# Output projection with its second half in two passes, two expert weight loads placed between them, and expert choice for two token tiles at a time

## The chip, the cores and the metric

The kernel runs on one core of one Trainium2 chip. The metric is the device time of one execution in microseconds (us); the result is the median over several runs. The engines are PE (TensorE, matrix products), PEld (its weight loads), DVE (VectorE), ACT (ScalarE), POOL (GpSimd) and SP (SyncE, which here only issues DMA transfers).

## The reference

One layer of a decoder trunk on 512 tokens of width 1024, all in float32. Only the middle of it matters here:

```python
x = x + (merged @ w_out)                     # output projection, 1024 x 1024
h = rmsnorm(x) * g_ffn
lg = h @ w_router_g + b_rg                   # 4 groups: the best one is taken
le = h @ w_router_e + b_re                   # 8 experts in each: the best two of that group
wts = p_g * softmax(top2(le[group]))
for each token, for its two experts e:       # 32 experts, hidden width 256
    out += (silu(h @ w_gate[e]) * (h @ w_up[e])) @ w_down[e] * wts
```

Ahead of it stand an input projection with attention, convolution and mLSTM branches; behind it a per-layer embedding and a last RMSNorm.

## The kernel before

The program is written engine by engine: each engine has one instruction stream in a fixed order, and semaphores tie the streams together. So every order spoken of below is written out by hand.

**Output projection.** `project(i)` computes, for i = 0 to 7, 512 output columns (half i // 4) of the token tile i % 4 of 128 tokens. Each operand is split into a rounded high part and a low remainder, so one tile takes 24 matrix products of 128x128 by 128x512: `by_part` lists them as high x high (part 0), high x low weights (part 1), low merged x high weights (part 2), 8 each. The four banks PA, PB, S_1 and S_4 take the tiles in turn. DVE adds the result to the residual (`add_x2`), PE transposes it (`turn_half`), DVE multiplies by the gain (`h2_half`) and PE computes the router's logits (`router`). All of that runs between pieces of the next tile's projection.

**Choice of experts.** `pick(t)` on DVE takes the logits of one tile: scale and bias, best group, mask, best two of 32, one-hot rows `oh`, and their sum `tmp`. `row_root` finishes the RMSNorm's reciprocal root with five small instructions ahead of it. PE counts tokens per expert from `tmp` (the banks RANKS for tiles 0 and 1, LAST_RANKS for tiles 2 and 3), DVE turns the counts into slots (`ranked`), PE sums a table of token numbers by slot (HIT), and DVE writes it out as `table`. POOL then gathers the tokens of each expert, 64 at a time, from the copy of x in memory (`x2_rows`). The weights of the tokens follow: a chain of small DVE instructions, and PE's products HIT_WEIGHT. Only behind these, in PE's order, stands the first `turn_block`, which transposes the gathered rows of expert 0.

**Experts.** Each of 32 experts loads 2048 KB (`up_weights`) and 1024 KB (`down_weights`). There are 7 places for up weights (`RING`) and 9 for down weights (`DOWN_RING`). They lie in memory that earlier stages used. Place 4 for up weights lies on `merged_low`, place 3 for down weights on the last four k tiles of `wo_low` for the second half, place 5 on `wo_high` of the second half, place 4 for down weights on the first four k tiles of its `wo_low`. SP issues the load of up n (n from 7 on) once `up_done` says that expert n - 7 has left its place. SP's stream after the projection's first half reads:

```python
            sp.wait_ge(x2_mm, T)
            up_weights(2)
            up_weights(3)
            ...
            sp.wait_ge(x2_mm, 2 * T)
            store_x2(T - 1)
            down_weights(3)
            down_weights(4)
            up_weights_in_halves(4)
            up_weights_in_halves(5)
```

Of the kernel before, what the change touches and what calls it, by code (L numbers as in the profile page):

```python
# [31 lines left out]
ALU = mybir.AluOpType  # L32
# [3 lines left out]
P = 128  # L36
# [87 lines left out]
def build(nc, x, consts, chan, g_mix, r_bias, g_final, w_cm, w_tm, w_if, w_gate, w_branch, w_out,  # L124
# [5 lines left out]
    with ExitStack() as ctx:  # L130
# [6 lines left out]
        def sem(name):  # L137
            return ctx.enter_context(nc.semaphore(name))
# [168 lines left out]
        best = sb("best", [P, T, 8])  # L307
        best_at = sb("best_at", [P, 8], mybir.dt.uint32)
        best_index = sb("best_index", [P, 8])
        ov = sb("ov", [P, 3, NEXP])  # L310
# [123 lines left out]
        wo_loaded = sem("wo_loaded")  # L434
        x2_mm = sem("x2_mm")
        x2_ready = sem("x2_ready")
        x2_squared = sem("x2_squared")
# [63 lines left out]
        def _(sp):  # L501
# [87 lines left out]
            up_weights(2)  # L589
            up_weights(3)  # L590

            def store_x2(t):
# [80 lines left out]
        def _(act):  # L673
# [288 lines left out]
            for i in range(2 * T):  # L962
# [6 lines left out]
                if i >= T:  # L969
# [3 lines left out]
                                   bias=mean_halves[:, t:t + 1]).then_inc(rooted, 1)  # L973
            act.wait_ge(picked, T)
            act.activation(t4[:, :, :], t4[:, :, :], ACT.Exp).then_inc(act_step, 1)
# [109 lines left out]
        def _(pe):  # L1085
# [249 lines left out]
            last_tile_last = sorted(by_part, key=lambda q: (q[1] == KD - 1, q))  # L1335

            def project(i, first=0, end=3 * KD):

                half, tokens = i // T, slice(i % T * P, (i % T + 1) * P)
                bank = (PA, PB, S_1, S_4)[i % 4]  # L1340
                if i >= T and first == 0:
                    pe.wait_ge(x2_ready, i - 3)
                if i == T:
                    pe.wait_ge(rounded, WO_REST_ROUNDED + KD)
                for n, (part, k) in list(enumerate(last_tile_last if i == 0 else by_part))[first:end]:
                    if i == 0 and part == 0:
                        pe.wait_ge(rounded, MERGED_ROUNDED + k + 1)
                    if i == 0 and part == 1 and k in (0, KD - 1):
                        pe.wait_ge(gate_split, WO_SPLIT + KD)
                    if i == 0 and part == 2:  # L1350
                        pe.wait_ge(gate_split, MERGED_SPLIT + k + 1)
                    if i == T and n == KD:
                        pe.wait_ge(gate_split, WO_REST_SPLIT + KD)
                    last = mm(bank[:, :], (merged_high, merged_high, merged_low)[part][:, k, tokens],
                              (wo_high[half][:, k, :], wo_low[:, half, k, :], wo_high[half][:, k, :])[part],
                              n == 0, n == 3 * KD - 1)
                if end == 3 * KD:
                    last.then_inc(x2_mm, 1)
# [39 lines left out]
            for i in range(1, T + 1):  # L1398
                project(i, 0, 4)
                turn_half(i - 1)  # L1400
                project(i, 4, 10)
                router(i - 1)
                project(i, 10)
            for i in range(T + 1, 2 * T):
                project(i, 0, 4)
                turn_half(i - 1)
                if i < 2 * T - 1:
                    project(i, 4, 10)
                else:
                    project(i, 4, 8)  # L1410
                    pe.wait_ge(picked, 2)
                    mm(RANKS, const("upper"), tmp[:, 0:2, :], True, False)
                    mm(RANKS[:, NEXP:], ones, tmp[:, 0, :], False, True).then_inc(routing_mm, 1)
                    project(i, 8, 10)
                router(i - 1)
                project(i, 10)

# [16 lines left out]
            for q in range(2):  # L1434
                mm(LAST_RANKS, ones, tmp[:, q, :].unsqueeze(1).to_broadcast([P, 2, NEXP]), q == 0, False)
            pe.wait_ge(picked, 3)
            mm(LAST_RANKS[:, NEXP:], ones, tmp[:, 2, :], False, False)

# [11 lines left out]
            constant_products(3)  # L1450
            pe.wait_ge(picked, T + 1)
            mm(LAST_RANKS, const("upper"), tmp[:, 2:T, :], False, True).then_inc(routing_mm, 1)
            constant_products(3)
# [64 lines left out]
            for n in range(NEXP):  # L1518
                pe.wait_ge(up_loaded[n % RING], (n // RING + 1 + (n % RING in (4, 5))) * 16)
# [85 lines left out]
        def _(dve):  # L1605
# [414 lines left out]

            def pick(t, meanwhile):

                of = lambda q: per[:, q, 0, t:t + 1]
                groups, experts, left = rl[:, t, 0:NGROUP], rl[:, t, NGROUP:], le[:, t, :]
                dve.wait_ge(logits_done, T + t + 1)
                chain(dve.scalar_tensor_tensor(rl[:, t, :], logits_in(t, 1), rr2[:, t:t + 1], r_b[:, :], ALU.mult, ALU.add))
                if t < T - 1:
                    chain(dve.scalar_tensor_tensor(rl[:, t, :], logits_in(t, 0), rr2[:, t:t + 1], rl[:, t, :], ALU.mult, ALU.add))
                first_max(groups, const("rev4"), oh4[:, t, :], of(1), of(11))
                last = dve.tensor_scalar(t4[:, t, :], groups, of(1), None, ALU.subtract)  # L2030
                if t == T - 1:
                    last.then_inc(picked, 1)
                chain(dve.tensor_scalar(oh4[:, t, :], oh4[:, t, :], of(11), 1.0, ALU.is_equal, ALU.subtract))
                chain(dve.scalar_tensor_tensor(left.rearrange("p (g e) -> p g e", g=NGROUP),
                                               spread(oh4[:, t, :], [P, NGROUP, PER_GROUP], 2), BIG,
                                               experts.rearrange("p (g e) -> p g e", g=NGROUP), ALU.mult, ALU.add))
                chain(dve.max(best[:, t, :], left))
                chain(dve.max_index(best_at[:, :], best[:, t, :], left))
                chain(dve.tensor_copy(best_index[:, 0:2], best_at[:, 0:2]))
                chain(dve.tensor_scalar(oh[:, 0, t, :], numbers, best_index[:, 0:1], None, ALU.is_equal))  # L2040
                meanwhile()
                dve.scalar_tensor_tensor(tmp[:, t, :], numbers, best_index[:, 1:2], oh[:, 0, t, :], ALU.is_equal, ALU.add)\
                   .then_inc(picked, 1)
                chain(dve.tensor_scalar(oh[:, 1, t, :], numbers, best_index[:, 1:2], None, ALU.is_equal))
                dve.tensor_tensor(entries_ids.rearrange("p (k t) w e -> p k t w e", k=2)[:, :, t],
                                  oh[:, :, t, :].unsqueeze(2).to_broadcast([P, 2, 2, NEXP]),
                                  const("ids").rearrange("p (k t w) -> p k t w", k=2, w=2)[:, :, t, :].unsqueeze(3)
                                  .to_broadcast([P, 2, 2, NEXP]), ALU.mult)

# [367 lines left out]
```

## Time and profile before

| | |
|---|---|
| median of 3 runs | 944.79 us |
| lowest, highest | 941.2 us, 945.15 us |
| span of the profiled execution, first to last instruction | 939.8 us |
| PE busy | 895.7 us (95%) |
| DVE busy | 497.7 us (53%) |
| ACT busy | 343.9 us (37%) |
| POOL busy | 194.1 us (21%) |
| bytes read, written | 175.33 MB, 12.59 MB |

The profiled execution has a span of 939.8 us. Its own device time is not listed beside it; the three timed runs lie 1.4 to 5.4 us above that span. A busy share is a mean over stages with different limits. The stages that matter here are the projection (574 to 630 us from the start), the choice of experts (630 to 648 us) and the experts (648 to 868 us).

### The profile page before, as it was taken

Reading aid. Unit: us, or ns where it says so; the run is one execution under the profiler, and the core shown is the slowest. Engines: PE = TensorE matmul, PEld = TensorE weight load, DVE = VectorE, ACT = ScalarE, POOL = GpSimd, SP = SyncE. Lnnn points to the kernel's source line nnn. Section 1 sums busy time; section 2 is a strip of 40 time slices with the busy share of each in tenths; the row PEclk is TensorE's granted clock in tenths of the full one; section 3 lists DMA queues with packets and bytes.
Section 4 is the critical chain, followed back from the end, with each engine's and each line's share of the span. In section 5 each row is a group of like instructions: output and inputs, shape, how many; then the busy total and the mean of one; then the engine's idle time right before and its main releaser. Section 6 shows DMA issues by size and latency. Waiting matters only on the chain. (4 is left out here: it accounts for less than half of the span.)

```text
span 939.8 us, 12274 instructions
## 1 busy us (share of the span) xinstructions
PE 895.7 (95%) x4824; PEld 656.4 (70%) x4824; DVE 497.7 (53%) x1039; ACT 343.9 (37%) x571; POOL 194.1 (21%) x169
## 2 busy tenths in 40 slices
PE   5999999999999999899999999997999999878897
PEld 4778788878877866788888888885555555433486
DVE  6378579758866978743333344374311221211766
ACT  5534453535445347622222234120222212112565
POOL 0052263327225332000000000002233233221000
PEclk9999999999999999999999999999999999999999
DMA  7520321222031110442222208959999999999801
GB/s 277 177 93 23 130 73 45 70 89 68 23 113 45 68 35 0 182 199 101 101 100 101 101 1 326 402 186 381 412 419 419 419 419 421 419 421 413 313 24 68
DMA packets 28657, 180.35 MB, mean 192 GB/s; under 512 B 5792, under 2 KB 6304, under 8 KB 17848
## 3 DMA queue, kind: packets, MB, share of 16 engines
q1 hardware_dynamic: 23480, 171.16, 46.4%
q0 software_dynamic: 5120, 8.41, 2.4%
q8 instruction: 39, 0.64, 0.3%
q14 instruction: 18, 0.15, 0.0%
HBM read 175.33 MB, written 12.59 MB: 200 GB/s over the span
## 5 line engine op out<-in xcount | busy, mean ns | idle before, releaser
L1087 PE MATMUL bank<-mT_parts,low_parts 128*128 128x512 f32 (+1 forms) x456 | 178.5, 394 | 0.0
L1087 PE MATMUL bank<-arena,cst 128*64 128x256 f32 (+2 forms) x920 | 134.1, 431 | 9.7 <-DMA arena<-in_w_expert 7.2
L1087 PE MATMUL bank<-mT_parts,x_parts 128*128 128x512 f32 (+1 forms) x328 | 132.5, 404 | 1.0 <-DVE low_parts L1676 1.0
L1087 PE MATMUL bank<-hT_parts,x_parts 128*128 128x512 f32 (+1 forms) x328 | 129.1, 394 | 0.0
L1676 DVE TENSOR_TENSOR low_parts<-arena,x_parts 128x1024 fp32r<-128x1024 f32 (+1 forms) x44 | 62.8, 1427 | 98.1 <-ACT x_parts L702 97.8
L2150 DVE TENSOR_TENSOR cst<-bank,chn 128x512 f32<-128x512 f32 x32 | 22.1, 692 | 166.7 <-PE bank L1480 166.7
L1087 PEld LDWEIGHTS bank<-arena,cst 128*64 128x64 f32 (+1 forms) x920 | 63.7, 138 | 65.1 <-issue 31.5
L1087 PEld LDWEIGHTS bank<-mT_parts,low_parts 128*128 128x128 f32 (+1 forms) x456 | 85.0, 186 | 21.2
L1728 DVE SCALAR_TENSOR_TENSOR arena<-arena,chn 128x512 f32<-128x512 f32 x116 | 99.2, 912 | 0.0
L2301 POOL DMA_INDIRECT mT<-x_rows,table x32 | 33.0, 1031 | 274.8 <-DVE table L2080 262.2
L1087 PE MATMUL bank<-arena 128*128 128x64 f32 (+9 forms) x400 | 79.9, 332 | 1.2 <-DVE small L1825 1.2
L2286 POOL TENSOR_TENSOR arena<-arena 128x128 f32<-128x128 f32 (+3 forms) x32 | 40.3, 1260 | 177.7 <-ACT arena L798 177.7
L1087 PEld LDWEIGHTS bank<-mT_parts,x_parts 128*128 128x128 f32 (+1 forms) x328 | 61.0, 186 | 17.0 <-DVE low_parts L1676 2.1
L1087 PEld LDWEIGHTS bank<-hT_parts,x_parts 128*128 128x128 f32 (+1 forms) x328 | 61.0, 186 | 15.1 <-issue 0.7
L1087 PEld LDWEIGHTS bank<-arena 128*128 128x128 f32 (+1 forms) x400 | 56.3, 189 | 21.5 <-issue 14.3
L2307 POOL DMA_INDIRECT expert_rows<-mT,table x32 | 32.4, 1014 | 150.9 <-ACT mT L995 146.3
L798 ACT ACTIVATE arena<-arena,small 128x384 f32<-128x384 f32 (+3 forms) x32 | 32.6, 1020 | 55.8 <-DVE small L1825 55.8
L1087 PE MATMUL bank<-mT_parts,cm_high_b 128*128 128x512 f32 x128 | 51.6, 412 | 0.0
L939 ACT ACTIVATE arena<-bank 128x512 f32<-128x512 f32 x24 | 14.2, 597 | 100.6 <-PE bank L1087 96.2
L1087 PE MATMUL bank<-hT_parts,cm_high_b 128*128 128x512 f32 x128 | 49.2, 393 | 0.0
L995 ACT ACTIVATE mT<-bank,table_weight 128x512 f32<-128x512 f32 x32 | 22.0, 687 | 67.0 <-PE bank L1087 67.0
L1087 PE MATMUL bank<-x_parts,mT_parts 128*128 128x384 f32 x128 | 44.6, 349 | 0.0
(300 smaller groups left out, 1574.7 us busy)
## 6 DMA issues: line engine op xcount, KB each, us to landing
arena<-in_w_expert SPq DMA_DIRECT2D x21, 2048.0 KB, 26.5
arena<-in_w_expert SPq DMA_DIRECT2D x26, 1024.0 KB, 23.7
arena<-in_w_cm SPq DMA_DIRECT2D x32, 512.0 KB, 3.6
arena<-in_w_gate SPq DMA_DIRECT2D x8, 1536.0 KB, 6.7
yT<-in_w_expert SPq DMA_DIRECT2D x5, 2048.0 KB, 22.9
hT<-in_w_expert SPq DMA_DIRECT2D x4, 2048.0 KB, 25.0
arena<-in_w_tm SPq DMA_DIRECT2D x4, 1536.0 KB, 7.0
arena<-in_w_branch SPq DMA_DIRECT2D x8, 768.0 KB, 8.2
```

Of the source, the lines that this page charges most:

```text
L798: act.activation(sc[:, u % 2, 0:n], sc[:, u % 2, 0:n], ACT.Exp, bias=nmx[:, u % 2:u % 2 + 1], accum_out=den[:, u:u + 1]).then_inc(exps_don ...
L939: act.activation(sgm[:, br], (PA, PB, S_16)[br][:, :], ACT.Sigmoid).then_inc(gate_read, 1)
L995: act.activation(yr[slot], Y[b2][:, :], ACT.Copy, scale=table_w(0, n)).then_inc(y_scaled, 1)
L1087: return pe.matmul(out, lhsT, rhs, start=start, stop=stop)
L1676: dve.tensor_tensor(low, weights, high.bitcast(F32), ALU.subtract).then_inc(done, 1)
L1728: dve.scalar_tensor_tensor(cacc[:, j % 2], ypad[:, j:j + SEQ], weight, cacc[:, j % 2], ALU.mult, ALU.add).then_inc(conv_step, 1)
L2150: dve.tensor_tensor(xT[b2], TR[:, :].rearrange("p (k h s) -> p k h s", k=KD // 2, h=2), chn[:, G_FFN:G_FFN + KD].rearrange("p (h k) -> p k ...
L2286: pool.tensor_tensor(dst[:, 0:n], sc[:, u % 2, 0:n], sc[:, u % 2, n:2 * n], ALU.add).then_inc(pool_step, 1)
L2301: pool.indirect_dma_start(out=xr[slot], out_offset=None, in_=x2_halves, in_offset=bass.IndirectOffsetOnAxis(ap=token_halves, axis=0), boun ...
L2307: pool.indirect_dma_start(out=expert_halves, out_offset=bass.IndirectOffsetOnAxis(ap=row_halves, axis=0), in_=yr[slot], in_offset=None, bo ...
```

## The change

The second half of the projection is done in two passes over its four tiles. The first pass does 12 of the 24 products of every tile (all of part 2, then k tiles 4 to 7 of part 1), and leaves four unfinished sums in the four banks. A new semaphore `low_mm` says that it is over; `merged_low` and half of `wo_low` are then free. SP waits for it right behind `up_weights(3)`, and issues `up_weights(4)` (now whole) and `down_weights(3)` there. The second pass does the other 12 products of each tile. `pick` takes two tiles at once, `pick(0)` and `pick(2)`: some of its instructions now cover both tiles, others stand there twice. The call for the first two tiles stands ahead of `add_x2` of the last tile; the last pair needs both roots and `ranked(0, ...)` ahead of it.

```diff
@@ SP @@
             sp.wait_ge(x2_mm, T)
             up_weights(2)
             up_weights(3)
+            sp.wait_ge(low_mm, 1)
+            up_weights(4)
+            down_weights(3)
...
             store_x2(T - 1)
-            down_weights(3)
             down_weights(4)
-            up_weights_in_halves(4)
             up_weights_in_halves(5)
@@ PE @@
+            low_first = [(2, k) for k in range(KD)] + [(1, k) for k in range(KD // 2, KD)]
+            second_half = low_first + [(1, k) for k in range(KD // 2)] + [(0, k) for k in range(KD)]
+            LOW = len(low_first)
...
+                if i == 2 * T - 1 and end == LOW:
+                    last.then_inc(low_mm, 1)
...
-                project(i, 10)
+                project(i, 10, LOW if i == T else 3 * KD)
             for i in range(T + 1, 2 * T):
-                project(i, 0, 4)
-                turn_half(i - 1)
...
-                router(i - 1)
-                project(i, 10)
+                project(i, 0, LOW)
+            project(T, LOW)
+            project(T + 1, LOW, LOW + 5)
+            turn_half(T)
+            project(T + 1, LOW + 5)
+            project(T + 2, LOW, LOW + 1)
+            router(T)
...
+            turn_half(T + 2)
+            project(T + 3, LOW + 5)
...
-            constant_products(2)
+            router(2 * T - 2)
             turn_half(2 * T - 1)
-            constant_products(1)
+            pe.wait_ge(picked, 2)
+            mm(RANKS, const("upper"), tmp[:, 0:2, :], True, False)
+            mm(RANKS[:, NEXP:], ones, tmp[:, 0, :], False, True).then_inc(routing_mm, 1)
             router(2 * T - 1)
@@ DVE, pick @@
+                chained_by_tile(lambda t: dve.scalar_tensor_tensor(rl[:, t, :], logits_in(t, 1), rr2[:, t:t + 1], r_b[:, :],
+                                                                   ALU.mult, ALU.add), tiles)
+                chained_by_tile(lambda t: dve.scalar_tensor_tensor(rl[:, t, :], logits_in(t, 0), rr2[:, t:t + 1], rl[:, t, :],
+                                                                   ALU.mult, ALU.add), [t for t in tiles if t < T - 1])
+                once_read()
+                chain(dve.tensor_reduce(of(1), groups, AXX, ALU.max))
...
+                chained_by_tile(lambda t: dve.max(best[:, t, :], le[:, t, :]), tiles)
+                chained_by_tile(lambda t: dve.max_index(best_at[:, t - first, :], best[:, t, :], le[:, t, :]), tiles)
...
+                dve.tensor_tensor(tmp[:, pair, :], oh[:, 0, pair, :], oh[:, 1, pair, :], ALU.add).then_inc(picked, 2)
@@ DVE, the calls @@
-            for t in range(T - 1):
-                h2_half(T + t)
-                row_root(t)
-                if t == T - 2:
-                    ranked(0, RANKS, 1)
-                pick(t, lambda: add_x2(T + t + 1))
+            h2_half(T)
+            add_x2(T + 1)
+            row_root(0)
+            h2_half(T + 1)
+            add_x2(T + 2)
+            row_root(1)
+            pick(0, lambda: h2_half(T + 2))
+            add_x2(T + 3)
...
             h2_half(2 * T - 1)
+            row_root(T - 2)
             row_root(T - 1)
-            pick(T - 1, lambda: None)
+            ranked(0, RANKS, 1)
+            pick(T - 2, lambda: None)
```

Two places in the order of instructions show what moves.

PE, from the last tile of the projection (512 columns wide, operands `wo_low`, `wo_high`, `merged_low`, `mT_parts`) to its router products (128x36), before:

```order
L1087 MATMUL bank<-wo_high_62,mT_parts 128x512 x4
L1087 MATMUL bank<-tmp,cst 128x64
L1087 MATMUL bank<-tmp,cst 128x32
L1087 MATMUL bank<-wo_low,mT_parts 128x512 x2
L1087 MATMUL bank<-wr_sb,cst 128x36 x4
L1087 MATMUL bank<-wo_low,mT_parts 128x512 x6
L1087 MATMUL bank<-wo_high_62,merged_low 128x512 x8
L1087 MATMUL bank<-cst 128x128 x2
L1380 MATMUL bank<-cst,x_sb 128x128 x4
L1087 MATMUL bank<-cst 128x128
L1087 MATMUL bank<-wr_sb,cst 128x36 x4
```

The same place in the changed program:

```order
L1389 MATMUL bank<-cst,x_sb 128x128 x4
L1089 MATMUL bank<-wo_high_62,mT_parts 128x512 x7
L1089 MATMUL bank<-wr_sb,cst 128x36 x4
L1389 MATMUL bank<-cst,x_sb 128x128 x4
L1089 MATMUL bank<-tmp,cst 128x64
L1089 MATMUL bank<-tmp,cst 128x32
L1089 MATMUL bank<-wr_sb,cst 128x36 x4
```

The third tile's router products and the two products into RANKS (128x64 and 128x32) now stand behind the last product of the projection, and the three constant products around the last transposes are gone.

DVE, from the last two pieces of `add_x2` (128x256) to the last tile's router row (`rl`), before:

```order
L1979 TENSOR_TENSOR x_sb<-x_sb,bank 128x256 x2
L2042 SCALAR_TENSOR_TENSOR tmp<-cst,best_index,oh 128x32
L2044 TENSOR_SCALAR oh<-cst,best_index 128x32
L2045 TENSOR_TENSOR cst<-oh,cst 128x2x64
L1989 TENSOR_TENSOR cst<-bank,chn 128x256 x2
L1637 TENSOR_SCALAR small<-small 128x1
...
L1645 TENSOR_TENSOR small<-small 128x1
L2026 SCALAR_TENSOR_TENSOR rl<-bank,small,r_b 128x36
```

The same place in the changed program:

```order
L2083 TENSOR_TENSOR cst<-oh,cst 128x2x64 x2
L1992 TENSOR_TENSOR x_sb<-x_sb,bank 128x256 x2
L2002 TENSOR_TENSOR cst<-bank,chn 128x256 x2
L1650 TENSOR_SCALAR small<-small 128x1
...
L1658 TENSOR_TENSOR small<-small 128x1
L2028 TENSOR_TENSOR rank_terms<-bank,oh 128x128
L2030 TENSOR_REDUCE per<-rank_terms 128x2x2
L2031 TENSOR_TENSOR cst<-per,cst 128x2x128
L2054 SCALAR_TENSOR_TENSOR rl<-bank,small,r_b 128x36 x2
L2056 SCALAR_TENSOR_TENSOR rl<-bank,small,rl 128x36
```

The whole of `pick(0)` stands ahead of the last `add_x2`, two `row_root` of five instructions stand behind it where there was one, and the three instructions of `ranked(0, ...)` have come in between them and the last pair's choice.

## Rows read from the trace of the kernel before

**Rows 1.** Timeline of SP's DMA issues (start us, us, engine, line), 630 to 653 us

```profile
630.60 0.32 SPq L594 DMA_DIRECT2D x_rows<-x_sb  x1
...
652.96 0.33 SPq L559 DMA_DIRECT2D arena<-in_w_expert  x1
```

**Rows 2.** Windows by stage: length, busy PE PEld DVE ACT POOL, granted clock, DMA share, GB/s

```profile
613.00:632.00 19.00, 18.55 (x100) 14.97 (x99) 15.29 (x68) 3.43 (x10) 0.00 (x0) 1.00 0.41 154
632.00:653.00 21.00, 16.99 (x145) 11.47 (x145) 10.40 (x45) 1.33 (x3) 5.25 (x5) 0.92 0.99 389
657.00:810.00 153.00, 153.00 (x1118) 79.26 (x1116) 31.25 (x82) 31.97 (x72) 48.04 (x47) 1.00 1.01 418
810.00:868.00 58.00, 46.22 (x302) 21.75 (x299) 7.67 (x20) 9.90 (x22) 12.10 (x12) 1.00 1.01 420
```

**Rows 3.** PE's timeline, 600 to 657 us; a product is recorded as one or two instructions

```profile
603.79 0.98 PE L1087 MATMUL bank<-wr_sb,cst 128*128 128x36 f32 x8
604.61 1.66 PE L1087 MATMUL bank<-wo_low,mT_parts 128*128 128x512 f32 x6
606.10 2.01 PE L1087 MATMUL bank<-wo_high,merged_low 128*128 128x512 f32 x8
607.95 1.10 PE L1087 MATMUL bank<-wo_high,mT_parts 128*128 128x512 f32 x4
...
635.62 0.43 PE L1087 MATMUL bank<-tmp,cst 128*128 128x64 f32 x2 [0.83 <-DVE tmp L2042]
...
637.21 0.69 PE L1087 MATMUL bank<-cst 128*64 128x64 f32 x16 [0.44 <-DVE cst L2018]
637.83 1.08 PE L1087 MATMUL bank<-tmp,cst 128*128 128x32 f32 x8
638.74 4.54 PE L1087 MATMUL bank<-cst 128*128 128x512 f32 x10
643.21 1.15 PE L1087 MATMUL bank<-mT,cst 128*64 128x64 f32 x32
646.23 0.66 PE L1480 MATMUL bank<-cst,mT 128*128 128x128 f32 x4 [1.86 <-DMA mT<-x_rows,table]
647.76 5.17 PE L1087 MATMUL bank<-arena,cst 128*64 128x256 f32 x32 [0.88 <-DVE cst L2150]
...
656.52 1.95 PE L1087 MATMUL bank<-yT,cst 128*64 128x256 f32 x16
```

**Rows 4.** Half-microsecond windows, the same columns: the granted clock, and the DMA queues run dry

```profile
648.00:648.50 0.50, 0.50 (x4) 0.32 (x4) 0.00 (x0) 0.00 (x0) 0.50 (x1) 0.50 1.00 393
...
653.00:653.50 0.50, 0.50 (x4) 0.27 (x3) 0.00 (x0) 0.49 (x1) 0.00 (x0) 1.00 0.19 74
```

**Rows 5.** DVE's timeline, 625 to 636 us

```profile
625.34 0.29 DVE L2015 TENSOR_TENSOR rank_terms<-bank,oh 128x128 f32<-128x128 f32 x1
...
626.37 0.26 DVE L2026 SCALAR_TENSOR_TENSOR rl<-bank,small,r_b 128x36 f32<-128x36 f32 x1
626.66 0.26 DVE L2028 SCALAR_TENSOR_TENSOR rl<-bank,small,rl 128x36 f32<-128x36 f32 x1
...
629.77 0.75 DVE L1979 TENSOR_TENSOR x_sb<-x_sb,bank 128x256 f32<-128x256 f32 x2 [0.59 <-PE bank L1087]
...
631.75 0.20 DVE L1637 TENSOR_SCALAR small<-small 128x1 f32<-128x1 f32 x1
...
632.74 0.26 DVE L2026 SCALAR_TENSOR_TENSOR rl<-bank,small,r_b 128x36 f32<-128x36 f32 x1
...
633.68 0.23 DVE L2030 TENSOR_SCALAR t<-rl,per 128x4 f32<-128x4 f32 x1
633.81 0.23 DVE L2033 TENSOR_SCALAR oh<-oh,per 128x4 f32<-128x4 f32 x1
...
635.31 0.25 DVE L2042 SCALAR_TENSOR_TENSOR tmp<-cst,best_index,oh 128x32 f32<-128x32 f32 x1
```

**Rows 6.** POOL's timeline: the first gather

```profile
639.13 1.26 POOL L2301 DMA_INDIRECT mT<-x_rows,table  x1 [262.18 <-DVE table L2080]
```

More of the change, by code:

```diff
@@ L435, in build @@
         x2_mm = sem("x2_mm")
+        low_mm = sem("low_mm")
         x2_ready = sem("x2_ready")
@@ L1342, in project @@
                     pe.wait_ge(x2_ready, i - 3)
-                if i == T:
+                if i == T and first == 0:
                     pe.wait_ge(rounded, WO_REST_ROUNDED + KD)
-                for n, (part, k) in list(enumerate(last_tile_last if i == 0 else by_part))[first:end]:
+                order = second_half if i >= T else last_tile_last if i == 0 else by_part
+                for n, (part, k) in list(enumerate(order))[first:end]:
                     if i == 0 and part == 0:
@@ L1402, in _ @@
                 router(i - 1)
-                project(i, 10)
+                project(i, 10, LOW if i == T else 3 * KD)
             for i in range(T + 1, 2 * T):
-                project(i, 0, 4)
-                turn_half(i - 1)
[L1407 to L1414, printed above, removed]
-                router(i - 1)
-                project(i, 10)
+                project(i, 0, LOW)
[5 more added lines that the diff above has]
+            router(T)
+            project(T + 2, LOW + 1, LOW + 5)
+            turn_half(T + 1)
+            project(T + 2, LOW + 5)
+            project(T + 3, LOW, LOW + 1)
+            router(T + 1)
+            project(T + 3, LOW + 1, LOW + 5)
+            turn_half(T + 2)
+            project(T + 3, LOW + 5)
             def constant_products(count):
@@ L1435, in _ @@
                 mm(LAST_RANKS, ones, tmp[:, q, :].unsqueeze(1).to_broadcast([P, 2, NEXP]), q == 0, False)
-            pe.wait_ge(picked, 3)
-            mm(LAST_RANKS[:, NEXP:], ones, tmp[:, 2, :], False, False)
             def hits(first, end, starts, stops):
@@ L1451, in _ @@
             pe.wait_ge(picked, T + 1)
+            mm(LAST_RANKS[:, NEXP:], ones, tmp[:, 2, :], False, False)
             mm(LAST_RANKS, const("upper"), tmp[:, 2:T, :], False, True).then_inc(routing_mm, 1)
@@ L2019, in ranked @@
                                   slots.unsqueeze(1).unsqueeze(1).to_broadcast([P, 2, 2, BLK]), ALU.is_equal).then_inc(slots_ready, 1)
[L2021 to L2031, printed above, removed]
-                    last.then_inc(picked, 1)
[L2033 to L2048, printed above, removed]
@@ new lines, in pick, with chained_by_tile @@
+            def pick(first, once_read):
+                tiles = range(first, first + 2)
+                pair = slice(first, first + 2)
+                of = lambda q: per[:, q, 0, pair]
+                of_tile = lambda q, t: per[:, q, 0, t:t + 1]
+                groups = rl[:, pair, 0:NGROUP]
+                rows_of = lambda ap, n: spread(ap, [P, 2, n], 2)
+                both = lambda ap, n: spread(ap, [P, 2, n], 1)
+                def chained_by_tile(make, on):
+                    for t in on:
+                        ins = make(t)
+                        if t < on[-1]:
+                            steps[0] += 1
+                            ins.then_inc(dve_step, 1)
+                    chain(ins)
+                dve.wait_ge(logits_done, T + first + 2)
+                chained_by_tile(lambda t: dve.scalar_tensor_tensor(rl[:, t, :], logits_in(t, 1), rr2[:, t:t + 1], r_b[:, :],
[4 more added lines that the diff above has]
+                chain(dve.tensor_reduce(of(1), groups, AXX, ALU.max))
+                last = dve.tensor_tensor(t4[:, pair, :], groups, rows_of(of(1), NGROUP), ALU.subtract)
+                if first:
+                    last.then_inc(picked, 1)
+                chained_by_tile(lambda t: dve.scalar_tensor_tensor(oh4[:, t, :], rl[:, t, 0:NGROUP], of_tile(1, t), const("rev4"),
+                                                                   ALU.is_equal, ALU.mult), tiles)
+                chain(dve.tensor_reduce(of(11), oh4[:, pair, :], AXX, ALU.max))
+                chained_by_tile(lambda t: dve.tensor_scalar(oh4[:, t, :], oh4[:, t, :], of_tile(11, t), 1.0,
+                                                            ALU.is_equal, ALU.subtract), tiles)
+                chained_by_tile(lambda t: dve.scalar_tensor_tensor(
+                    le[:, t, :].rearrange("p (g e) -> p g e", g=NGROUP), spread(oh4[:, t, :], [P, NGROUP, PER_GROUP], 2), BIG,
+                    rl[:, t, NGROUP:].rearrange("p (g e) -> p g e", g=NGROUP), ALU.mult, ALU.add), tiles)
+                chained_by_tile(lambda t: dve.max(best[:, t, :], le[:, t, :]), tiles)
+                chained_by_tile(lambda t: dve.max_index(best_at[:, t - first, :], best[:, t, :], le[:, t, :]), tiles)
+                chain(dve.tensor_copy(best_index[:, :, 0:2], best_at[:, :, 0:2]))
+                for k in range(2):
+                    last = dve.tensor_tensor(oh[:, k, pair, :], rows_of(best_index[:, :, k], NEXP), both(numbers, NEXP),
+                                             ALU.is_equal)
+                    if k == 0:
+                        steps[0] += 1
+                        last.then_inc(dve_step, 1)
+                chain(last)
+                dve.tensor_tensor(tmp[:, pair, :], oh[:, 0, pair, :], oh[:, 1, pair, :], ALU.add).then_inc(picked, 2)
+                for t in tiles:
+                    dve.tensor_tensor(entries_ids.rearrange("p (k t) w e -> p k t w e", k=2)[:, :, t],
+                                      oh[:, :, t, :].unsqueeze(2).to_broadcast([P, 2, 2, NEXP]),
+                                      const("ids").rearrange("p (k t w) -> p k t w", k=2, w=2)[:, :, t, :].unsqueeze(3)
+                                      .to_broadcast([P, 2, 2, NEXP]), ALU.mult)
```

8 lines of the change are left out of this document (4 added, 4 removed).

## The prediction

> **What bounds the kernel now.** I read the windows by stage first, since the 95% of the page mixes stages. From 657 to 810 us both PE and the DMA engines are full, and from 810 to 868 us only DMA is: PE falls to 46.2 of 58 us while DMA stays at 420 GB/s [rows 2]. The two resources don't have the same work: an expert costs PE about 6.3 us and DMA 3072 KB of weights (3.15 MB) plus about 0.5 MB of gathered and scattered rows, 3.67 MB / 0.418 = 8.7 us. So PE uses up its lead of loaded weights until 810 us, and the stage ends when the last bytes have come. In the stage before it, 613 to 632 us, DMA is used to 41% [rows 2]. The tempting account is this: 3 MB of weights moved into that hole are 3.15 MB / 0.42 = 7.5 us less behind it.
>
> The SP timeline says otherwise. After its loads of 631 to 636 us SP issues nothing until 652.96 [rows 1]: all 7 places are taken, and it waits until expert 0's up products are over. Those start at 647.76 and last 5.17 [rows 3]: 652.93. In that half microsecond the DMA share is 0.19 [rows 4]: the queue has run dry. It is full again soon after, and stays so to the end. So the last byte's time is the moment at which place 0 comes free, plus a fixed number of bytes. Filling the ring sooner only makes the wait for that moment longer. **What counts is when expert 0's up products end.** I call it T0, 652.9 us before.
>
> What sets T0? Going back: a wait for the first gather until 646.23, with 1.86 us of idle PE in it, issued by POOL at 639.13 [rows 3, 6]; ahead of that `table`, and DVE without a gap from 629.77 on [rows 5].
>
> **The loads (worth nothing by themselves).** `low_mm` comes about 12.5 us into the second half, near 613.5 us. Up 4 and down 3 then take 7.5 us of idle DMA. What is left after the last store (630.60 before [rows 1]) is down 4, up 5, down 6 and the store itself, 4.5 MiB, 4.7 MB / 0.42 = 11.2 us: from 631.5 to about 642.8 us instead of 652. The stores of x follow SP's new wait. The first of them is ready after it anyway (its sum needs 12 more products), so the wait holds up nothing.
>
> **PE's order.** 96 products of 0.231 us (606.10 to 607.95 for eight [rows 3]) stay 96. One router (603.79 to 604.61, 0.82 us) and the RANKS pair (like the 0.43 at 635.62) leave the stretch [rows 3], so the last sum is complete 1.2 to 1.9 us sooner than the 629.77 at which DVE took it [rows 5], near 628.2. That would be a gain, if DVE took it then.
>
> **DVE takes it later.** `pick(0)` waits for the second tile's router. Behind that router PE has eleven products (2.5 us) and a transposition (0.5) until the last sum: 628.2 - 3.0 = 625.2, with the root 625.4. One tile's choice takes 2.57 us from its first row to `tmp` (632.74 to 635.31). The other half's row adds 0.29 (626.37 to 626.66). A second independent instruction of the same form starts 0.13 behind its first (633.68, 633.81) [rows 5]; I take 0.14. Eight such seconds, and 0.1 for the double index search, are 1.2 us. With `tmp`, two `entries_ids` and the `h2_half` inside (0.55 + 0.6) the pair takes 5.2 us: `add_x2` of the last tile at 630.6, **+0.9** against 629.77. Its cover is gone: PE has only a router and then nothing until these sums.
>
> **Behind the last sum**, all on DVE and in one chain:
> - a second `row_root`, 631.75 to 632.74 [rows 5]: **+1.0**
> - `ranked(0)`, formerly beside the projection, 625.34 to 626.37 [rows 5]: **+1.0**
> - the pair in place of one tile: 7 x 0.14 + 0.29 + 0.1: **+1.3**
>
> Together `table` is 4.2 us later. The 31 DVE instructions that the pairs save lie where DVE had time.
>
> **What is given back.** PE's HIT_WEIGHT products ended at 643.21 + 1.15 = 644.36 and then PE waited 1.86 us for the gather [rows 3]. Now they end at 648.6. The gather is issued at 643.3. Its landing is not shown with empty queues: the 7.1 us from 639.13 to 646.23 [rows 3, 6] stood behind full ones and are the upper end (650.4); the lower end is 0 for what PE would notice. I take 0, since the queues drain by 642.8. The Trainium skill, "DMA: Bandwidth & Descriptors", section "Anatomy of one DMA - SWDGE (gpsimd) path", fits 2.0 us plus bytes / 436e3 for such a transfer: an estimate of 2.6 us for 256 KB, by which it lands near 646; by the row's 7.1 us the total would be 1.8 us longer.
>
> So expert 0's transposition starts at 648.6 instead of 646.23: +2.4. And its up products ran at a granted clock of 0.50, which is 1.2 GHz [rows 4], after PE had idled from 644.4: 5.17 us where the same number of products at 2.4 GHz takes 2 x 1.95 = 3.9 [rows 3]. PE now comes to them from 6 us of unbroken products, so I count -1.3. Sum: **+1.1 us** if the clock never falls.
>
> **The clock ahead of it.** From 628.5 to 641 us PE has, by the sums above, some 4 us of work in 12.5, with two stretches of about 2.5 us without any (628.7 to 631.1, 637.2 to 639.7). Before, 1.86 us idle followed by little work cost the clock [rows 3, 4]. If it falls, the pieces on the chain double at most: router 0.98, ranks 0.43, hits 0.69, totals 1.08 [rows 3], together 3.2; lower end 0. I take 1.4, near the middle, since the clock may come back between. Total **+2.5 us: 947.3 us**. The durations are those of one execution with a span of 939.8 us, under the median of 944.79 by 5.0; I add the difference to the median. A measurement of this kernel can tell about 0.5% (4.7 us) from no change.
>
> **Rivals.**
> 1. **The clock stays down into the fillers** (slower). The five filler products take 4.54 us at 2.4 GHz [rows 3] and cover DVE's chain of the weights. At 1.2 GHz they need up to 9 us and stand between that chain and HIT_WEIGHT: with the chain's 3.2 and up to 3 of the fillers, +1.1 + 2.5 + 2.5 = about +6, 951 us. It decides if PE comes to the fillers, near 643 us, at clock 0.5. For it: PE's two long gaps. Against it: in the old gaps at 635 us the clock held. The Trainium skill, "TensorE: Matmul & The Clock Gate", section "The HAM clock gate", speaks for it: the slow clock is the default state there, and sustained activity lifts it.
> 2. **The bytes count after all** (faster): if the ring is not what holds the DMA, the whole 7.5 us come off: 937.3. Against it stand the share of 0.19 at 653 us and the issue at 652.96 [rows 1, 4].
> 3. **The pairs cost less than I count**, or the freed DMA speeds the gather and the spilled rows more: the 4.2 us shrink to 3 with no clock loss, -0.1: 944.7. The duration of two-tile forms is not in the trace.
> 4. **The gather stays slow**: 7.1 us even with empty queues. Expert 0 starts at 650.4, +4.2, and PE idles again and loses the clock as before: 949.0.
>
> **Chances.** Forecast 0.45, rival 1 0.20, rival 2 0.10, rival 3 0.15, rival 4 0.10. Faster by over 0.5% is rival 2: 0.10. Slower by over 0.5% (from 949.5) is most of rival 1 (0.18), half of rival 4 (0.05) and the top of the forecast's own spread (0.05): 0.28. The rest is 0.62. The range takes in the forecast, rivals 3 and 4 and most of rival 1, and at its lower end the spread of the three runs (lowest 941.2, 3.6 below the median): 941.5 to 951.8. Rival 2 stays out.
>
> **What would show it.** Right: SP's two loads issued near 613.5; the last `add_x2` near 630.6, directly behind `pick(0)`; `table` near 642.3; DMA idle for some 8 us around 648; SP's next issue near 654 to 656, as much later than 652.96 as the total is longer; PE without waits for weights until about 810 us. Wrong: a last up load that lands sooner although SP's first ring issue is later (then bytes bound the stage, rival 2), or a `table` at 638, which would take away every plus above.

## The result, and the profile after

| | before | after |
|---|---|---|
| median of nine runs each, taken side by side | 943.62 us (938.98 to 945.15) | 947.66 us (944.48 to 949.11) |
| ratio, 95% interval | | 1.0046 [1.0030, 1.0062] |
| span of the profiled execution | 939.8 us | 942.7 us |
| mean granted clock of that execution | 0.995 | 0.986 |

The change costs 4.3 us (2.8 to 5.9, the ratio times 943.62). That is more than nothing and less than the 0.5% that the prediction took as its bound. Executions of one kernel differ too: 75 of the kernel before, made beside the experiments, lie between 939.1 and 945.9 us, the quarter with the longest times at a mean granted clock of 0.989 and the shortest at 0.995; each trace shows one execution.

The two executions do not run in step. The same instruction, the fourth `add_x2`, starts at 601.15 before and at 599.62 after, so **1.53 us have to be added to a time of after** to compare it with one of before. "Aligned" below always means this: times are counted from that instruction in each trace.

The page of the changed kernel, its busy time by engine:

```profile
span 942.7 us, 12245 instructions
...
PE 901.1 (96%) x4818; PEld 662.0 (70%) x4818; DVE 493.7 (52%) x1025; ACT 343.9 (36%) x571; POOL 194.5 (21%) x169
```

PE shows 5.4 us more than the 895.7 of before. The windows by stage say where (the columns of [rows 2]):

```profile
613.00:632.00 19.00, 16.67 (x94) 14.27 (x92) 12.01 (x52) 6.40 (x14) 0.00 (x0) 0.95 0.87 295
632.00:653.00 21.00, 18.81 (x119) 13.64 (x121) 12.62 (x58) 0.67 (x3) 5.23 (x5) 0.64 0.65 258
653.00:657.00 4.00, 3.40 (x31) 2.31 (x26) 0.56 (x1) 1.10 (x1) 0.04 (x1) 1.00 0.31 68
657.00:810.00 153.00, 152.72 (x1113) 79.12 (x1113) 33.43 (x92) 31.84 (x73) 47.15 (x46) 1.00 1.01 416
```

Beside [rows 2] three things have changed. The DMA share from 613 to 632 us rose from 0.41 to 0.87: the hole is filled. From 632 to 653 us it fell from 0.99 to 0.65: what was moved forward is missing here. And in the same 21 us PE's busy time rose from 16.99 to 18.81 although it ran fewer products (119 recorded against 145), with a granted clock of 0.64 instead of 0.92. From 657 to 810 us nothing differs by more than 1% in PE or DMA.

SP's issues (start, length, engine, line):

```profile
630.30 0.45 SPq L568 DMA_DIRECT2D arena<-in_w_expert  x1
630.79 1.31 SPq L565 DMA_DIRECT2D arena<-in_w_expert  x2
635.57 0.33 SPq L568 DMA_DIRECT2D x_sb<-in_w_expert  x1
655.85 0.33 SPq L560 DMA_DIRECT2D arena<-in_w_expert  x1
```

The last row answers to 652.96 in [rows 1]: the first issue that waits for a place of the ring. It comes 4.42 us later, aligned (655.85 + 1.53 - 652.96). The last expert's down product starts at 866.48 after and at 863.62 before, which is 4.39 later, aligned. The whole loss exists by T0, and is carried unchanged through some 210 us.

DVE's timeline, the last sum to `cc`:

```profile
629.12 0.75 DVE L1992 TENSOR_TENSOR x_sb<-x_sb,bank 128x256 f32<-128x256 f32 x2
630.13 0.92 DVE L2002 TENSOR_TENSOR cst<-bank,chn 128x256 f32<-128x256 f32 x2 [0.27 <-PE bank L1389]
630.97 0.20 DVE L1650 TENSOR_SCALAR small<-small 128x1 f32<-128x1 f32 x1
...
631.92 0.21 DVE L1650 TENSOR_SCALAR small<-small 128x1 f32<-128x1 f32 x1
...
632.87 0.29 DVE L2028 TENSOR_TENSOR rank_terms<-bank,oh 128x128 f32<-128x128 f32 x1
...
633.86 0.41 DVE L2054 SCALAR_TENSOR_TENSOR rl<-bank,small,r_b 128x36 f32<-128x36 f32 x2
...
637.63 0.23 DVE L2081 TENSOR_TENSOR tmp<-oh 128x64 f32<-128x64 f32 x1
...
641.51 0.28 DVE L2122 TENSOR_SCALAR table<-bank,cst 128x64 int32<-128x64 f32 x1 [1.38 <-PE bank L1089]
...
643.35 0.19 DVE L2125 COPY cc<-bank 128x32 f32<-128x32 f32 x1 [1.55 <-PE bank L1089]
```

From 629.12 to 637.63 only one row has a wait in brackets, `h2_half` with 0.27 us for the last transposition: DVE is the bound there, as the prediction had it. Behind that the brackets name PE's products. PE's timeline over the same stretch:

```profile
629.59 1.01 PE L1389 MATMUL bank<-cst,x_sb 128*128 128x128 f32 x4 [2.33 <-DVE x_sb L1992]
...
631.10 1.90 PE L1089 MATMUL bank<-wr_sb,cst 128*128 128x36 f32 x8
...
641.40 1.92 PE L1089 MATMUL bank<-tmp,cst 128*128 128x32 f32 x8
643.12 6.47 PE L1089 MATMUL bank<-cst 128*128 128x512 f32 x10
649.53 1.15 PE L1089 MATMUL bank<-mT,cst 128*64 128x64 f32 x32
650.61 0.65 PE L1493 MATMUL bank<-cst,mT 128*128 128x128 f32 x4
652.14 3.67 PE L1089 MATMUL bank<-arena,cst 128*64 128x256 f32 x32 [0.88 <-DVE cst L2192]
```

The router's products (x8 in the row) take 1.90 where before they took 0.98, the totals (128x32) 1.92 for 1.08, the fillers (128x512) 6.47 for 4.54 [rows 3]. Only expert 0's up products got faster: 3.67 for 5.17. Windows of 3 us on the changed kernel show the granted clock (third number from the right) behind it:

```profile
627.00:630.00 3.00, 0.67 (x6) 0.42 (x6) 2.62 (x15) 0.10 (x1) 0.00 (x0) 0.99 0.96 229
630.00:633.00 3.00, 3.00 (x16) 3.00 (x16) 2.52 (x13) 2.20 (x4) 0.00 (x0) 0.50 0.97 381
633.00:636.00 3.00, 2.90 (x24) 2.60 (x25) 2.72 (x15) 0.22 (x1) 0.00 (x0) 0.50 1.03 427
636.00:639.00 3.00, 1.79 (x9) 1.50 (x8) 2.09 (x15) 0.21 (x1) 0.00 (x0) 0.50 1.02 429
639.00:642.00 3.00, 3.00 (x26) 2.66 (x26) 1.29 (x4) 0.00 (x0) 0.00 (x0) 0.50 1.04 434
642.00:645.00 3.00, 3.00 (x10) 1.97 (x10) 1.48 (x6) 0.00 (x0) 1.98 (x2) 0.50 0.58 225
645.00:648.00 3.00, 3.00 (x6) 1.36 (x5) 2.69 (x12) 0.00 (x0) 2.28 (x3) 0.66 0.39 118
648.00:651.00 3.00, 3.00 (x40) 1.78 (x38) 0.77 (x4) 0.00 (x0) 0.00 (x0) 1.00 0.12 32
```

PE was idle for 2.33 us ahead of 629.59; from 630 to 647 us the granted clock is 0.50 (1.2 GHz), and it is back at 1.00 (2.4 GHz) from 647 on, while the fillers run without a break from 643.12. Before, it is 1.00 in each such window up to 645. The rule of the Trainium skill by which rival 1 was argued ("TensorE: Matmul & The Clock Gate", section "The HAM clock gate": slow is the default, sustained activity lifts it) agrees with this trace in that the clock fell behind idle PE and rose while the fillers ran without a break. That slow is the default no run here shows.

### The profile page after: what moved, and what is told of

It reads as the page before. It is cut to its first block and busy times, and to the rows that moved or that the text cites. A ratio compares the mean times of both kernels' runs of the same rounds, so it can differ in the third digit from the quotient of the medians.

```text
span 942.7 us, 12245 instructions
## 1 busy us (share of the span) xinstructions
PE 901.1 (96%) x4818; PEld 662.0 (70%) x4818; DVE 493.7 (52%) x1025; ACT 343.9 (36%) x571; POOL 194.5 (21%) x169
```

## The experiments

All measured differences are the ratio times the 942 to 944 us of the kernel before on the same chip, with the 95% interval behind. "T0" is SP's first issue into the ring. Each diff is against the kernel named. What was expected of 3, 5, 7 and 8 was written with the results of 1, 2, 4 and 6 known, and of 9 and 10 with all the others. Each kernel has one trace.

**1. The loads alone** (against after): up 4 and down 3 are issued where they were before.

```diff
             up_weights(3)
-            sp.wait_ge(low_mm, 1)
-            up_weights(4)
-            down_weights(3)
...
+            down_weights(3)
             down_weights(4)
+            up_weights(4)
```

> The changed kernel with up 4 and down 3 loaded again behind the projection's end (up 4 as one transfer), all else as changed. Theory 1, the end of expert 0's up products sets the time: that moment stays where it is in the changed kernel (about 4.4 us later in the program than before), because the 7.3 MB then in the queues are through near 648 us and the first gather lands near 650 us, just as PE comes to it; so +4.3 us against before, like the change itself, within 1 us. Theory 2, the bytes set the time and the change gained 7.5 us by its early loads while it lost about 12 elsewhere: +11.8 us against before.

Measured +5.7 us (3.6 to 7.7), where after has +4.3 (2.8 to 5.9). T0 is 655.45:

```profile
655.45 0.33 SPq L560 DMA_DIRECT2D arena<-in_w_expert  x1
```

Counted from the fourth `add_x2` (599.46 here) that is 0.24 us sooner than in after. **3 MB issued 18 to 19 us earlier (612.2 and 612.5 us in after) bring nothing that these runs can tell from zero**: the medians put 1.4 us between the two kernels, which is within their noise, and the traces 0.1. The theory by which bytes count wanted some 7.5 us between them, and falls. That holds for a PE that comes late: in this kernel the gather was issued at 642.65, and PE had no wait for it at 650.22, 7.57 us later.

**2. and 3. PE's idle stretches filled** (against after): products of constants ahead of the last transposes and, more than the three there were, behind the hits of tiles 0 and 1. Twelve stood in that second place first, then eight.

```diff
             router(2 * T - 2)
+            constant_products(8)
             turn_half(2 * T - 1)
...
-            constant_products(3)
+            constant_products(12)
```

> The changed kernel with 8 constant products of 128x128 ahead of the last transposes and 12 in place of 3 behind the first hits, so that PE has no long gap. Theory 1: the granted clock stays at 1.0 (2.4 GHz); the pieces of PE on the chain and the five fillers lose what the clock of 0.50 cost them, about 4.0 us, and expert 0's up products end about 3.7 us sooner than in the changed kernel: +0.6 us against before, within 1. Theory 2, the clock in that stretch hides beside DVE's chain: +4.3 us, as the change. If the added products are too long they delay the last transposes by up to 0.5 us.

> The changed kernel with 8 constant products in each of the two gaps; the run before with 12 in the second gap delayed the ranks by 1.0 us and still fell to the slow clock from 635 to 638 us. Theory 1: expert 0's up products end 1.0 us sooner than there if the clock is as it was (+0.7 us against before, within 1), and up to 1 us later than that if the shorter filling costs the clock longer: not above +2.

Measured +1.7 us (-0.1 to 3.4) with twelve, +1.6 (0.1 to 3.2) with eight. Windows of the kernel with eight:

```profile
630.00:633.00 3.00, 2.47 (x20) 2.20 (x20) 2.47 (x13) 2.30 (x4) 0.00 (x0) 1.00 0.96 382
633.00:636.00 3.00, 1.86 (x24) 1.79 (x24) 2.71 (x14) 0.22 (x1) 0.00 (x0) 0.87 1.06 415
636.00:639.00 3.00, 3.00 (x16) 2.79 (x16) 2.23 (x15) 0.21 (x1) 0.00 (x0) 0.56 0.99 404
639.00:642.00 3.00, 2.56 (x31) 2.25 (x31) 1.41 (x5) 0.00 (x0) 0.00 (x0) 1.00 1.01 423
```

Products that compute nothing take 2.7 us off the changed kernel (1.0046 against 1.0017; about 0.6 to 4.8 by the two intervals), and T0 comes 3.4 sooner, aligned. The clock is up except for some 3 us around 637; both kernels came out about 1 us above the +0.6 and +0.7 expected, and this rest of half clock is one reason. With twelve, the ranks of the last pair also waited about 1 us behind them.

**4. Tile by tile** (against after): the two passes stay, `pick` takes one tile again; the logits of both tiles are scaled first. (`pick` as in the kernel before; its diff is long.)

```diff
-            pick(0, lambda: h2_half(T + 2))
+            scale_logits(0)
+            scale_logits(1)
+            h2_half(T + 2)
+            pick(0)
+            pick(1)
...
-            pick(T - 2, lambda: None)
+            scale_logits(T - 2)
+            scale_logits(T - 1)
+            pick(T - 2)
+            pick(T - 1)
```

> The changed kernel with both passes and the early loads, but the experts chosen tile by tile as before (the logits of both tiles of a pair are still scaled first). Theory 1: the pairs are not what costs; two single choices take 5.9 us where the pair takes 3.6, so the last add is 2.3 us later and the last tmp 2.2 us more: +4.3 + 4.5 = +8.8 us against before. Theory 2, the pairs themselves cost the time (their last tile waits for its neighbour): this kernel falls back to between 0 and +2 us.

Measured +10.7 us (8.5 to 12.8), 6.3 more than after and 1.9 more than expected. About 1 us of that is again the clock: the fillers, at half clock for longer, took 7.43 us, where after has 6.47. So the pairs are not what costs: they take back 6 us of what the two passes do. Given that the routers come together at the end, choosing two tiles at once is right; what is lost on DVE is lost because two tiles are still open there at all.

**5. Expert 0 late, nothing else** (against before): nine products of constants, 128x512, ahead of the first `turn_block`.

```diff
+            for q in range(9):
+                mm(Y[0][:, :], ident, cst[:, 0:512])
             turn_block(0, 0, rows_gathered[0], 16, first=True)
```

> The kernel before with nine constant products of 128x512 on PE ahead of expert 0's first transposition, about 8.1 us of work of which 1.9 fill the old wait for the gather; no byte and nothing on DVE changes. PE comes to expert 0 at 652.5 us and its up products end near 657.7 instead of 652.9, at full clock. Theory 1, that moment sets the time: +4.8 us. Theory 2, the bytes set it and PE, which has a lead of weights until 810 us, catches up: 0.

```profile
644.33 7.99 PE L1087 MATMUL bank<-cst 128*128 128x512 f32 x18
652.16 0.60 PE L1480 MATMUL bank<-cst,mT 128*128 128x128 f32 x4
653.64 3.67 PE L1087 MATMUL bank<-arena,cst 128*64 128x256 f32 x32 [0.87 <-DVE cst L2152]
```

Measured +5.8 us (4.0 to 7.8); T0 is 657.34, 4.35 later aligned. The delay alone, in the kernel before, makes a loss like that of the change (+4.3, 2.8 to 5.9). As in after, up products at full clock (3.67) give part of the delay back.

**6. The last tile alone in two passes** (against before): only the last tile does its low parts first, up 4 and down 3 follow near 626 us. Routers, choices and roots stay.

```diff
+            sp.wait_ge(low_mm, 1)
+            up_weights(4)
+            down_weights(3)
             sp.wait_ge(x2_mm, 2 * T)
             store_x2(T - 1)
-            down_weights(3)
             down_weights(4)
-            up_weights_in_halves(4)
```

> The kernel before with one thing of the change: in the last tile of the projection alone the low parts come first, and up 4 and down 3 load behind them, near 625 us, in place of 631 us. The choice of experts stays beside the projection, tile by tile, as before. Theory 1: table stays at 638 us, the queues are through near 644 instead of 652 us, the first gather lands up to 1.8 us sooner, PE does not idle and keeps its clock for expert 0 (1.3 us): between -1.5 and -3.1 us against before. Theory 2, the bytes set the time: -5 us, the idle DMA time from 625 to 631 us that is filled. Theory 3, early loads are worth nothing in any order: 0.

Measured +2.4 us (0.6 to 4.2), a gain had been expected. The trace (SP, POOL, PE) shows a wait I had not thought of:

```profile
629.82 0.33 SPq L595 DMA_DIRECT2D x_rows<-x_sb  x1
...
638.85 0.33 SPq L568 DMA_DIRECT2D x_sb<-in_w_expert  x1
...
639.79 1.26 POOL L2310 DMA_INDIRECT mT<-x_rows,table  x1 [263.39 <-DMA x_rows<-x_sb]
...
647.64 1.11 PE L1489 MATMUL bank<-cst,mT 128*128 128x128 f32 x4 [4.06 <-DMA mT<-x_rows,table]
```

The last store of x, issued at 629.82 some 3.5 us behind 3 MB of loads, has landed by 638.85, when SP may issue down 6. DVE wrote `table` at 637.16, but POOL's gather is held until the store is in: it is issued 2.63 us behind `table`, where 1.18 passed before. The gather's landing then takes 7.85 us. PE idles 4.06 us and comes to expert 0 at half clock.

**7. Gather first** (against kernel 6): only up 4 stays early; down 3 and 4 follow the last store, and up 5 and down 6 are issued once the first gather has landed.

```diff
             up_weights(4)
-            down_weights(3)
             sp.wait_ge(x2_mm, 2 * T)
             store_x2(T - 1)
+            down_weights(3)
             down_weights(4)
+            sp.wait_ge(rows_gathered[0], 16)
             up_weights_in_halves(5)
```

> As the kernel with the last tile's low parts first, but only up 4 loads early; behind the last store come down 3 and down 4, and up 5 and down 6 wait until the first gather has landed. The run before showed that the two early loads delayed the landing of the last store (issued 629.8, landed about 638.8), which POOL waits for ahead of its gather, and that a gather beside full queues takes 7 to 8 us. Theory 1, expert 0's end sets the time: the gather starts with table at once, lands before PE is ready for it, expert 0's up products end about 3.2 us sooner than before, at full clock: -2.9 us against before, within 1. Theory 2, the DMA hole at 639 to 643 us is paid in full because the bytes set the time: 0. Theory 3, a gather takes 7 us whatever the queues hold: about -0.5.

```profile
641.77 0.81 SPq L565 DMA_DIRECT2D arena<-in_w_expert  x2
...
648.19 0.33 SPq L560 DMA_DIRECT2D arena<-in_w_expert  x1
```

Measured -1.6 us (-3.0 to -0.3): **faster than both kernels**, by little more than half of the 2.9 expected. POOL issues the gather at 637.50 and PE comes to the rows without a wait:

```profile
642.65 0.66 PE L1490 MATMUL bank<-cst,mT 128*128 128x128 f32 x4
644.49 3.67 PE L1090 MATMUL bank<-arena,cst 128*64 128x256 f32 x32 [1.18 <-DVE cst L2160]
```

SP, which waits for the same gather, issues up 5 at 641.77: it landed in 4.27 us at most, and the clock is not lost. T0 comes 3.2 sooner, aligned. Half of that is given back: the last down product comes 212.3 us after T0 instead of 210.7. The likely cause is the hole that the held loads left (the DMA share is 0.49 from 639 to 641 us).

**8. The hold alone** (against before).

```diff
             up_weights_in_halves(4)
+            sp.wait_ge(rows_gathered[0], 16)
             up_weights_in_halves(5)
```

> The kernel before, and only the two loads up 5 and down 6 wait for the first gather. Down 3, down 4 and up 4 (4.2 MB) with the store are through near 642 us, the gather lands near 643.5 instead of 646, PE is ready at 644.4: expert 0's up products end near 650. But the held 3.1 MB and the gathers then need DMA until about 653, so the ring is full no sooner than before: theory 1 gives -1 to 0 us; a gather of 7 us whatever the queues hold gives 0 to +1 (the hole is lost).

Measured -0.3 us (-1.8 to 1.1). T0 comes 1.6 sooner, aligned, and the distance grows to 213.0: one pays for the other. PE still waited for the gather, and this time kept its clock:

```profile
644.44 0.66 PE L1481 MATMUL bank<-cst,mT 128*128 128x128 f32 x4 [1.71 <-DMA mT<-x_rows,table]
645.97 3.67 PE L1088 MATMUL bank<-arena,cst 128*64 128x256 f32 x32 [0.87 <-DVE cst L2151]
```

So nearly all of the 1.6 is the 1.5 us that expert 0's up products save at full clock; the transposition ahead of them starts only 0.14 sooner, aligned.

**9. and 10. Kernel 7 without its hold, and with half of it** (against kernel 7): up 5 waits for nothing, or only its second half waits.

```diff
-            sp.wait_ge(rows_gathered[0], 16)
             up_weights_in_halves(5)
```

```diff
+            half_of_up_weights(5, 0)
             sp.wait_ge(rows_gathered[0], 16)
-            up_weights_in_halves(5)
+            half_of_up_weights(5, 1)
```

> As the run with the held loads (up 4 early in the last tile, all else as before), but up 5 and down 6 no longer wait for the first gather. If the hold is what makes the gather fast, it takes 7 us or more again, expert 0's up products end where they did before, and the early load by itself is worth nothing: 0 against before, within 1. If the early load alone is what gained, -1.6 as in that run.

> As the run with the held loads, but the first half of up 5 (1 MB, 2.5 us of DMA) goes ahead of the wait, to fill the hole of 639 to 644 us. In all kernels with a full ring the last expert's down products started 210.6 to 211.3 us after SP's first ring issue, with the held loads 212.3: the ring was not full. Theory 1 (both limits meet): the gather is still in time or less than 1 us late, the distance falls to 211: -2 to -3 us against before. Rival: the gather meets the extra megabyte and is 2 us late: -1 or less.

Without the hold: +1.9 us (0.7 to 3.2), where 0 within 1 had been expected; its trace has +0.8. With half of it: -0.7 (-2.0 to 0.6). Their first `turn_block`, first the one without:

```profile
645.21 0.66 PE L1489 MATMUL bank<-cst,mT 128*128 128x128 f32 x4 [2.23 <-DMA mT<-x_rows,table]
```

```profile
646.22 0.65 PE L1490 MATMUL bank<-cst,mT 128*128 128x128 f32 x4 [1.61 <-DMA mT<-x_rows,table]
```

The gathers were issued at 637.76 and 639.39: they took 7.45 and 6.83 us, PE waited in both, and expert 0's up products ran at half clock (5.36 us in both). So kernel 7 needs both its early load and its hold: without the hold it is 3.5 us slower, and the hold alone (kernel 8) brought nothing clear of the noise. Half of the hold did not make the gather fast: 1 MB more ahead of the gather keeps its landing at 6.8 us, while the queues still run dry behind it (share 0.20 from 645 to 647 us). I had expected -2 to -3 of the half; its rival (a gather 2 us late, -1 or less) came true.

All eleven kernels in one table. Both columns of differences are against before; "trace" is the change of T0 (aligned) plus that of the distance from T0 to the last expert's down product, 210.66 before.

| kernel | T0, aligned | distance | trace | measured |
|---|---|---|---|---|
| after | +4.42 | 210.63 | +4.4 | +4.3 (2.8 to 5.9) |
| 1 loads back | +4.18 | 210.75 | +4.3 | +5.7 (3.6 to 7.7) |
| 2 gaps filled, 12 | +1.72 | 210.94 | +2.0 | +1.7 (-0.1 to 3.4) |
| 3 gaps filled, 8 | +0.98 | 210.77 | +1.1 | +1.6 (0.1 to 3.2) |
| 4 tile by tile | +10.14 | 210.86 | +10.3 | +10.7 (8.5 to 12.9) |
| 5 expert 0 late | +4.35 | 210.56 | +4.3 | +5.8 (3.9 to 7.8) |
| 6 last tile only | +2.67 | 211.30 | +3.3 | +2.4 (0.6 to 4.2) |
| 7 gather first | -3.17 | 212.27 | -1.6 | -1.6 (-3.0 to -0.3) |
| 8 hold alone | -1.64 | 213.03 | +0.7 | -0.3 (-1.8 to 1.1) |
| 9 kernel 7, no hold | +0.53 | 210.90 | +0.8 | +1.9 (0.7 to 3.2) |
| 10 kernel 7, half a hold | -0.07 | 210.62 | -0.1 | -0.7 (-2.0 to 0.6) |

The distance is 210.6 to 211.3 us in every kernel but two. It grows only in 7 and 8, where all of up 5 was held back for the gather; with half of it held (10) it did not.

## Why the prediction was right

The forecast of 947.3 us, the range and the side (within 0.5%) held. The total is nearer than its steps deserve: the kernel before measured 943.62 beside the new one, 1.2 under the 944.79 that the forecast started from, and the loss was 4.3 where +2.5 had been given. Step by step, aligned:

| step | taken | measured |
|---|---|---|
| last `add_x2` late behind `pick(0)` | +0.9 | +0.88 |
| second root and `ranked(0)`, up to the pair's router row | +2.0 | +1.77 |
| pair in place of one tile, to `tmp` | +1.3 | +1.20 |
| clock: products from `tmp` to `table` | | +1.24 |
| clock: totals, to `cc` | | +0.84 |
| clock: fillers, to HIT_WEIGHT | | +1.92 |
| clock, the three together | +1.4 | +4.00 |
| wait for the gather gone | -1.8 | -1.94 |
| expert 0's up products at full clock | -1.3 | -1.50 |
| T0 | +2.5 | +4.42 |

Of the 1.24 some 0.1 is not the clock: a product for the counts of tile 2, done ahead of `tmp` before, now stands behind it. (At full clock, in kernel 2, PE's ranks take 0.59 us until DVE reads them, 638.97 to 639.56; before they took 0.47.)

**The chain on DVE** was sized to a quarter of a microsecond in each step. All of it came from rows of before: five small instructions, three of `ranked`, and 0.14 for a second instruction beside its first. The row at 633.86 shows the last of these: two of them in 0.41 where one took 0.26. Two figures of the prediction were wrong and entered no term: the pairs save 14 DVE instructions (1039 to 1025 on the pages), not 31. And 3.67 / 0.418 is 8.8, not 8.7.

**The loads at nothing** was right, and shown by experiment 1 to within about 2.6 us by the times and to 0.1 by the traces. A DMA share of 0.19 at T0 was the row that decided it against the 41% of the stage ahead.

**The gather's landing taken as covered** was right: PE has no wait at 650.61. Nothing here shows the 2.6 us that the prediction estimated by the fit of the Trainium skill ("DMA: Bandwidth & Descriptors", section "Anatomy of one DMA - SWDGE (gpsimd) path"); the shortest bound is the 4.27 us of experiment 7.

**The step that failed is the clock ahead of expert 0**: "I take 1.4, near the middle, since the clock may come back between". It did not come back between. It fell once, behind the first of the two idle stretches, and stayed down for 17 us, with PE busy in 13.7 of the first 15. So the small products took 1.8 to 1.9 times as long. Of the 3.2 named as the upper end the router's 0.98 was covered by DVE (no wait at 633.86), the rest came nearly in full (1.24 + 0.84), and the fillers cost 1.92 more, which the forecast had at nothing. PE's work was also put too low, at some 4 us: from 630 to 642 us it is busy for 10.7 us at half clock, which is over 5 at full. The condition of **rival 1** was thus fulfilled (PE came to the fillers at 643.12 at a clock of 0.50), and only its price of up to 3 us and its 951 us were too high: the clock rose while the fillers ran, and they took 6.47 and not 9 us. In size the truth lay between the forecast and rival 1, which had 0.20; in mechanism it was rival 1. The clock term was 2.6 us too small; that some 0.7 of it was made up by the other terms, and 1.2 by the lower median, is luck. Experiments 2 and 3 confirm the cause: work without any use in the two stretches took back 2.7 us by the times and 3.4 of T0 in the trace.

Rival 2 (bytes) is refuted by experiments 1 and 5. Rival 3's smaller price of the pairs did not come about. Rival 4 (7.1 us with empty queues) did not come true here, where PE had no wait, and is refuted by the 4.27 of experiment 7. What stays open: whether filling the gaps completely, or giving DVE's second root and `ranked(0)` another place, would bring the changed kernel to the one before; it wasn't tried.

## What to carry to other kernels

When a ring of buffers is full and its DMA queues have run dry by the time the first place comes free, the time of that first release sets the end, and bytes loaded sooner were worth nothing here: read the DMA share at that moment, not the mean of the stage ahead. Before work is batched or moved to the end of a stage, look at what it leaves to PE: idle stretches that cost nothing where they stand can cost the products behind them half their clock, as here. A load that is issued early shares the DMA engines with the store and the gather that the critical chain waits for, and holding it back until the gather has landed was here worth more than issuing it early.

## What the runs showed that I had not expected

- The clock stayed at 0.50 from 630 to 647 us while PE was busy for 13.7 of the 15 us from 630 to 645. Small products between short waits did not lift it here; it rose while the fillers ran.
- The length of a wait alone did not decide whether the clock fell. Ahead of expert 0, PE waited 1.86 us before, 2.23 in kernel 9 and 1.61 in kernel 10, and ran the up products in 5.17 to 5.36 us; in kernel 8 it waited 1.71 and ran them in 3.67. So a gain or loss of 1.5 us here can differ from one kernel to the next for a reason that these traces do not show.
- The first gather (issue by POOL to PE's first use) took 7.10 us before, 7.85 in kernel 6 and 7.45 in kernel 9, all with the queues full; 6.93 in kernel 8 (issued at 637.51) and 6.83 in kernel 10 (639.39), where they drained between 643 and 644 us; at most 5.15 in kernels 2 and 3 (642.62 and 642.08), where they drained at about the same time; and at most 4.27 in kernel 7 (637.50), where they drained from 638.5 us on.
- A store of x issued 3.5 us after 3 MB of loads was complete 9.0 us after its issue at the latest (629.82 to 638.85).
- The distance of 210.6 to 211.3 us from the ring's first issue to the last expert's down product held over ten kernels, the one before among them, whose T0 differ by 10 us.
